# Attention's products sorted and alternated between halves of TensorE's array, and the last expert pair's combine cut into column halves

## What is computed

```python
q, k, v, bg, u = _project(_rms(hp, norm1_g[l]), w_in[l], q_norm_g[l], k_norm_g[l])
att = _window_attention_prompt(q, k, v, sinks[l])      # 8 heads, 2 kv heads, chunks of 64 rows,
                                                       # each reads its own and the 2 chunks before
h = x + jnp.concatenate([att, conv_out], axis=-1) @ w_out
hn = _rms(h, norm2_g)
# for each expert e, over the rows that chose it:
gu = xe @ w_gu[e] + b_gu[e]
g = jnp.minimum(g, SWIGLU_LIMIT)
u = jnp.clip(u, -SWIGLU_LIMIT, SWIGLU_LIMIT)
h = (u + 1) * (g * jax.nn.sigmoid(SWIGLU_ALPHA * g))
y = h @ w_down[e] + b_down[e]                          # times the gate, added to the row of h
```

## Time and profile before

| | us |
|---|---|
| median of 3 runs | 1123.23 |
| the runs | 1122.68, 1123.23, 1125.21 |
| the profiled execution, as timed | 1125.32 |
| its span, first to last instruction | 1123.6 |
| PE busy | 1033.0 (92%) |
| DVE, ACT, POOL busy | 306.3, 102.2, 9.6 |
| weights and activations moved by DMA | 421.19 MB |

### The profile page before, as it was taken

The page is one execution under the profiler, slowest core; times in us unless marked ns, Lnnn a source line. Parts: engine busy times, 40 slices in busy tenths (PEclk is TensorE's granted clock), DMA queues, the critical chain, the costliest instruction groups (busy, mean ns, idle before and its releaser), DMA issues.

```text
span 1123.6 us, 11715 instructions
## 1 busy us (share of the span) xinstructions
PE 1033.0 (92%) x5061; PEld 492.3 (44%) x5062; DVE 306.3 (27%) x467; ACT 102.2 (9%) x172; POOL 9.6 (1%) x23
## 2 busy tenths in 40 slices
PE   5999999999999997989898999989898979898786
PEld 4766556443535442524343344434342524343332
DVE  2543121123132231231313032323231221313132
ACT  2122021100000000000001000000000000001010
POOL 1100000000000000000000000000000000000000
PEclk9999998999999999999999999999999999999998
DMA  9920536999999999999999999999999999999993
GB/s 338 338 93 1 224 126 257 420 422 420 422 421 421 421 421 421 421 421 421 421 422 421 421 421 421 421 421 420 421 421 421 421 421 421 422 421 422 420 422 144
DMA packets 61348, 421.19 MB, mean 375 GB/s; under 512 B 6776, under 2 KB 7084, under 8 KB 12112
## 3 DMA queue, kind: packets, MB, share of 16 engines
q1 hardware_dynamic: 60208, 418.93, 90.7%
q0 software_dynamic: 576, 1.34, 0.4%
q10 hardware_dynamic: 512, 0.15, 0.1%
HBM read 418.81 MB, written 1.58 MB: 374 GB/s over the span
## 4 chain that ended last, share of the span: by engine, by line
PE 60%; DMA 38%; SPq 1%; DVE 0%; issue 0%; DVEq 0%; ACT 0%
DMA ring<-in_w_gu_dram 29%; PE ps L721 24%; PE ps L736 8%; DMA ring<-in_w_down_dram 8%; PE ps L671 7%; PE ps L592 5%; PE ps L613 3%; PE ps L762 2%; PE ps L494 2%; PE ps L747 2%; DMA w_qkv<-in_w_in_dram 1%; PE ps L564 1%; SPq L356 1%; PE ps L621 1%; PE ps L723 1%; PE ps L765 1%
## 5 line engine op out<-in xcount | busy, mean ns | idle before, releaser
L721 PE MATMUL ps<-ring,xT 128*64 128x512 f32 x1024 | 458.1, 597 | 45.9 <-DMA ring<-in_w_gu_dram 45.7
L723 PE MATMUL ps<-ring,xT 128*64 128x512 f32 x1024 | 459.3, 598 | 0.0
L721 PEld LDWEIGHTS ps<-ring,xT 128*64 128x64 f32 x1024 | 133.9, 137 | 323.7 <-issue 319.8
L736 PE MATMUL ps<-ring,he 128*64 128x512 f32 x480 | 215.7, 595 | 18.2 <-DMA ring<-in_w_down_dram 17.9
L738 PE MATMUL ps<-ring,he 128*64 128x512 f32 x480 | 216.5, 596 | 0.0
L1358 DVE TENSOR_TENSOR x<-ps,x 128x512 f32<-128x512 f32 (+1 forms) x90 | 57.9, 683 | 339.0 <-PE ps L762 307.0
L723 PEld LDWEIGHTS ps<-ring,xT 128*64 128x64 f32 x1024 | 133.9, 137 | 0.0
L736 PEld LDWEIGHTS ps<-ring,he 128*64 128x64 f32 x480 | 62.4, 137 | 151.7 <-issue 151.1
L671 PEld LDWEIGHTS ps<-oh,hn 128*128 128x128 f32 x768 | 93.5, 198 | 6.2 <-issue 4.0
L671 PE MATMUL ps<-oh,hn 128*128 128x128 f32 x768 | 95.1, 282 | 0.0
L738 PEld LDWEIGHTS ps<-ring,he 128*64 128x64 f32 x480 | 62.4, 136 | 0.0
(11 more groups left out here) (197 smaller groups left out, 610.5 us busy)
## 6 DMA issues: line engine op xcount, KB each, us to landing
ring<-in_w_gu_dram SPq DMA_DIRECT2D x256, 1024.0 KB, 26.7
ring<-in_w_down_dram SPq DMA_DIRECT2D x128, 1024.0 KB, 27.3
w_chc<-in_w_in_dram SPq DMA_DIRECT2D x1, 4096.0 KB, 13.0
w_qkv<-in_w_in_dram SPq DMA_DIRECT2D x1, 3072.0 KB, 15.5
w_b<-in_w_in_dram SPq DMA_DIRECT2D x1, 2048.0 KB, 18.3
w_o<-in_w_out_dram SPq DMA_DIRECT2D x2, 1024.0 KB, 21.7
w_o<-in_w_out_dram SPq DMA_DIRECT2D x1, 2048.0 KB, 23.5
x<-in_x_prompt_dram SPq DMA_DIRECT2D x1, 1024.0 KB, 5.3
```

Of the source, the lines that this page charges most:

```text
L721: even = mm(gu_banks(j)[0:CAP, n, :], xT[j % 2][:, k, 0:CAP], ring[:, first % RING, cols], start=(k == 0), stop=(k == KT - 1))
L723: odd = mm(gu_banks(j)[CAP:P, n, :], xT[j % 2][:, k, CAP:P], ring[:, second % RING, cols], start=(k == 0), stop=(k == KT - 1))
L736: even = mm(out[0:CAP, half, :], hid[:, f, 0:CAP], ring[:, first % RING, cols], start=(f == 0), stop=(f == FT - 1))
```

## The change

**Attention.** `scores` loops over jp outside and g inside, so that successive products go to the two row halves; each g's last product tells `scores_done` (the count that DVE waits for is doubled). `attend` sorts the key tiles by size, the larger first, takes each tile through all four b before the next, and alternates g inside.

```diff
-                for b in range(4):
-                    g, jp = b // 2, b % 2
+                parts = sorted(key_tiles(c), key=lambda p: p[1] - p[2])
+                last = [None] * NKV
+                for i, (tile, k0, k1) in enumerate(parts):
+                    for jp, g in itertools.product(range(2), range(NKV)):
...
+                        b = 2 * g + jp
+                        last[g] = mm(AO[cols, jp * P:(jp + 1) * P], vals, probsT[k0:k1, tile, b * P:(b + 1) * P],
+                                     start=(i == 0 and jp == 0), stop=(i == len(parts) - 1), skip_group_check=True)
```

```diff
+            def keep_left():
+                pe.wait_ge(added, 2 * NT * (PAIRS - 2))
+                pe.wait_ge(u_biased, PAIRS)
+                pe.wait_ge(x_padded, 1)
+                for t in range(NT):
+                    mm(ps[:, LAST_BANK[2 * t], :], ident[:, :], x[:, t, 0:HALF], start=True, stop=False,
...
+            for half in range(2):
+                pe.wait_ge((front_yh, yh_ready)[half], (1, PAIRS)[half])
+                scatter_last(y_hi, ohT_last, half, False, False)
+                pe.wait_ge((front_yl, yl_ready)[half], (1, PAIRS)[half])
+                scatter_last(y_lo, ohT_last, half, False, True)
...
+            A(y_hi[:, 0:HALF], Y_LAST[:, 0, :], ACT.Copy, scale=gate_row[:, 0:1]).then_inc(front_yh, 1)
...
+            A(y_hi[:, HALF:D], Y_LAST[:, 1, :], ACT.Copy, scale=gate_row[:, 0:1]).then_inc(yh_ready, 1)
+            for t, (_, n) in enumerate(TT):
+                act.wait_ge(scattered, 2 * NT * (PAIRS - 2) + t + 1)
+                nc.scalar.copy(x[0:n, t, 0:HALF], ps[0:n, LAST_BANK[2 * t], :]).then_inc(front_added, 1)
+            act.wait_ge(front_added, 2)
...
+            sp.wait_ge(added, ADDED_LATE + NT + 2)
+            sp.dma_start(out_rows[:, :, HALF:D], x[:, 0:2, HALF:D]).then_inc(y_stored, 16)
+            sp.wait_ge(added, ADDED_LATE + NT + 3)
+            sp.dma_start(y_sample[0][:, HALF:D], x[0:DEC, 2, HALF:D]).then_inc(y_stored, 16)
```

More of the change, by code:

```diff
@@ L1 @@
+import itertools
 from contextlib import ExitStack
@@ L554, in attend @@
                     pe.wait_ge(att_mixed, c)
[L555 to L559, removed]
+                parts = sorted(key_tiles(c), key=lambda p: p[1] - p[2])
+                last = [None] * NKV
+                for i, (tile, k0, k1) in enumerate(parts):
+                    for jp, g in itertools.product(range(2), range(NKV)):
+                        cols = slice(g * HEAD_DIM, (g + 1) * HEAD_DIM)
                         if c == SAMPLE:
@@ L563, in attend @@
                             vals = v_nat[k0:k1, tile, cols]
-                        last = mm(AO[cols, jp * P:(jp + 1) * P], vals, probsT[k0:k1, tile, b * P:(b + 1) * P],
-                                  start=(i == 0), stop=(i == len(parts) - 1))
-                last.then_inc(att_done, 1)
+                        b = 2 * g + jp
+                        last[g] = mm(AO[cols, jp * P:(jp + 1) * P], vals, probsT[k0:k1, tile, b * P:(b + 1) * P],
+                                     start=(i == 0 and jp == 0), stop=(i == len(parts) - 1), skip_group_check=True)
+                for g in range(NKV):
+                    last[g].then_inc(att_done, 1)
             def turn_keys():
@@ L809, in _ @@
                 for m in range(DNC):
+                    if j == PAIRS - 1 and m == DNC - 1:
+                        keep_left()
                     down(j - 1, m)
@@ L820, in _, with scatter_last @@
             L = PAIRS - 1
[L822 to L826, removed]
+            def scatter_last(y, to, half, start, stop):
+                for t in range(NT):
+                    last = mm(ps[:, LAST_BANK[2 * t + half], :], to[:, t * P:(t + 1) * P],
+                              y[:, half * HALF:(half + 1) * HALF], start=start, stop=stop, skip_group_check=True)
                     if stop:
@@ L837, in _ @@
                     turn_oh(PAIRS)
[L838 to L845, removed]
+                else:
+                    if m == 1:
+                        pe.wait_ge(yl_ready, L)
+                        pe.wait_ge(ohT_ready, PAIRS)
+                    scatter_last(y_hi, ohT, m - 1, m == 2, False)
+                    last = scatter_last(y_lo, ohT, m - 1, False, False)
+            last.then_inc(last_but_one, 1)
+            down_last()
+            for half in range(2):
+                pe.wait_ge((front_yh, yh_ready)[half], (1, PAIRS)[half])
+                scatter_last(y_hi, ohT_last, half, False, False)
+                pe.wait_ge((front_yl, yl_ready)[half], (1, PAIRS)[half])
+                scatter_last(y_lo, ohT_last, half, False, True)
+            pe.wait_ge(front_added, NT)
             def again(n, e):
-                pe.wait_ge(added, n * 2 * NT + 2 * NT * (PAIRS - 2))
+                pe.wait_ge(added, n * 2 * NT + ADDED_LATE)
                 pe.wait_ge(oh_ready, n + PAIRS)
@@ L1411, in _ @@
             dve.wait_ge(last_but_one, 1)
-            split_yl(PAIRS, Y_LAST)
-            for u in range(2 * NT):
-                add_rows(2 * NT * (PAIRS - 2), u, LAST_BANK[u])
+            for half in range(2):
+                dve.wait_ge((front_yh, yh_ready)[half], (1, PAIRS)[half])
+                cols = slice(half * HALF, (half + 1) * HALF)
+                V.scalar_tensor_tensor(out=y_lo[:, cols], in0=Y_LAST[:, half, :], scalar=gate_row[:, 0:1],
+                                       in1=y_hi[:, cols], op0=ALU.mult, op1=ALU.subtract
+                                       ).then_inc((front_yl, yl_ready)[half], 1)
+            for t, (_, n) in enumerate(TT):
+                dve.wait_ge(scattered, 2 * NT * (PAIRS - 2) + NT + t + 1)
+                V.tensor_tensor(x[0:n, t, HALF:D], ps[0:n, LAST_BANK[2 * t + 1], :], x[0:n, t, HALF:D], ALU.add
+                                ).then_inc(added, 1)
             def next_round(q):
```

85 lines of the change are left out of this document (60 added, 25 removed).

## The result

| | before | after |
|---|---|---|
| median, us | 1123.22 (1122.68 to 1125.21, 4 runs) | 1112.79 (1111.64 to 1115.35, 4 runs) |
| profiled execution, us | 1125.32 | 1115.35 |
| its span, us | 1123.6 | 1113.6 |

The ratio is 0.9904, with a 95% interval of 0.9883 to 0.9925: faster by 10.4 us, where 9.3 was forecast.

What follows compares the result with a forecast made beforehand. It took the expert weight stream as the bound, its start set by TensorE's earlier work. Attention 5.6, scatter 0.2 and tail 3.5 made 9.3 us: 1123.23 - 9.3 = 1113.9 us, range 1111.2 to 1117.8.

Steps and rivals of the forecast that it cites:

- The bound: Expert weight stream, 421 GB/s: each microsecond taken from TensorE between 50 and 180 us brings the end forward by one.
- Attention, 5.6 us: `attend` of chunks 2, 3 and 4 from 2.89 to 1.18 us each, 5.1 us; chunk 4's scores, 0.5 us.
- Other engines: Softmax on DVE and ACT stays hidden under projection blocks; TensorE gets no new wait for it.
- keep_left: Three identity products before pair 14's last chunk pair: 2.6 us, just hidden by two chunk waits of together 2.63 us.
- Scatter of pair 14, 0.2 us: Pair 15's second chunk pair taken at landing, before the scatter products; down products end at 1110.8 instead of 1110.99 us.
- The cut of the last chunks: Loading the last two chunks in halves gains nothing and costs nothing, since TensorE is still last there.
- The tail, 3.5 us: After the last down product: 2.2 us up to the last add, 1.3 us from reading counts while stores fly.
- The adds: DVE adds only three blocks at the end; the last ends 4.6 us after the down products, before 6.8.
- the read's 1.3 us: SyncE reads the counts while the stores fly, not after; 1.3 us gained, last landing kept at 3.9 us after issue.
- Its lower bound of 2.5 us: Least gain at the end: two queues write at once in half-length rows, last landing a microsecond later.
- The clock: Half clock for 3.4 us at 124 us may vanish: zero against the median, 1.7 us against the profiled execution.
- The number: Whole-kernel median falls by 9.3 us, from 1123.23 to 1113.9 us; the forecast has chance 0.78.

Runs made afterwards that it cites:

- counts_first: Kernel before, with SyncE's wait for the stores moved behind its read of the counts; 1122.0 us, ratio 0.9993.
- read_early: Changed kernel, with SyncE reading the largest count ahead of its stores instead of behind them; 1113.37 us, ratio 0.9937.

## Why the prediction was right, point by point

- **The bound**: the stream lasted 921.2 us before and after, and each gain ahead of it reached the end. Right, and the main reason why the forecast came close.
- **Attention, 5.6 us**: 3 x 1.72 + 0.44 = 5.6. Right in each piece, and with the right mechanism: nothing was gained where two halves already ran beside each other. It was the sort, not the alternation; the forecast had worked the sum from the sorted blocks.
- **Other engines**: no new wait of TensorE for DVE or ACT up to the output projection.
- **keep_left**: 2.6 us forecast, 2.84 measured, hidden. The second chunk pair behind it, 15.0, started 0.14 us after its landing.
- **Scatter of pair 14, 0.2 us**: 15.1 was taken at its landing, as forecast, but the gain did not come. The down products end 4.2 us after the last landing, as before; the same work from 15.1 on took 13.98 us (1089.83 to 1103.81), where the sum had 13.7. The cut of the last chunks did nothing, right; but the forecast took the stream to end before 1106 us, and its last chunk landed at 1106.74.
- **The tail, 3.5 us**: 2.85. The adds were right (4.6 forecast, 4.7 measured). Of the read's 1.3 us I kept 3.9 us for the last landing, and it took 4.6. That term was mis-sized, by 0.7 us. Its lower bound of 2.5 us had room for a late landing, put down to two queues and half rows; `counts_first` has neither and lands nearly as late, 4.5 us after issue.
- **The clock**: counted at zero against the median, and at 1.7 us against the profiled execution, which without the fall at 124 us should have taken 1114.3 us. It had no such fall and took 1115.35: 0.65 us more in the tail, 0.2 for the scatter and 0.2 for the later first projection block. So what the profiles show of the change is 5.6 + 2.85 = 8.45 us, 0.85 less than forecast.
- **The number**: the median moved by 10.4 us, 1.1 more than forecast, and in the second measurement, on one chip with the variants, by 7.6 (1120.47 to 1112.83 us). The mechanism was right in both; that 9.3 came as close as it did to the first is in part luck, since half clock and start move a run by more than these differences, and the four runs of each kernel don't show where they lay.

## What to carry to other kernels

When a stream of weights is the bound, read what restarts it: here every microsecond of TensorE's work ahead of it counted, and `keep_left`, put into the waits inside it, cost nothing. Small products that use half the array cost most where kinds alternate; group them by kind first, and check in the timeline whether the halves already start together before changing their order. At an end that a processor bounds and not the last load, fill its last waits first.

## What the runs showed that was not expected

- Products of the free half start even behind two products (four passes) of the other half; behind four products they did not. Chunk 4's scores took 1.53 us in g-by-g order and 1.09 us alternated.
- A half-array product that follows one of the other kind costs 0.36 us (2.89 / 8) where in a group of its kind it costs 0.15 (0.59 / 4).
- SyncE's read of one value took 0.47 to 0.48 us where no store was under way (before, `read_early`) and 1.3 us behind stores.
- SyncE's last store landed 4.5 to 4.8 us after issue where SyncE went on to its branch, 3.9 to 4.0 where it waited.
- Runs of one kernel spread by 8.5 us, 0.8%. Two profiles of the changed kernel differ by 3.2 us through half clock ahead of the stream, and by 1.1 us the other way through the start of the first projection block.
